# A hybrid transformer block: x given a second time by channel, parameters as one array of columns

## The chip, the cores and the metric

The kernel runs on one core of a Trainium2 chip. The metric is the device time of one execution in microseconds. Engines are written as the profile writes them: PE (TensorE), PEld (its weight loads), DVE (VectorE), ACT (ScalarE), POOL (GpSimd), SP (SyncE, which here only issues transfers).

## The reference, cut to what matters

One decoder block on x of 512 tokens by 2048 channels, float32. The first part, which the change touches:

```
h      = x * rsqrt(mean(x*x over channels) + EPS) * mix_pre_g      # RMSNorm
proj   = h @ w_in                                                  # 2048 -> 7168
a_in, b_in, gates = split(proj)
a      = causal_depthwise_conv(a_val * sigmoid(a_gate), conv_a_w, 31 taps) + conv_a_b
a      = silu(layernorm(a) * ln_a_g + ln_a_b);   y_a = a @ w_a_out
y_b    = (causal pooling of b_in, one 256x256 map per group) * pool_scale @ w_b_out
x      = x + rmsnorm((sigmoid(g_a)*y_a + sigmoid(g_b)*y_b) @ w_o, mix_post_g)
```

Then come a gated MLP (2048 to 2 x 5632 and back, convolution of 3 taps, GELU) and a gated per-layer embedding, each with RMSNorm before or after it and a residual sum. Output: 512 by 2048 float32.

## The kernel before, in words

Every float32 product is made of three matmuls on float32r operands: each operand is split into a high part (rounded by ACT) and a low part (the rest, subtracted by DVE), and PE computes high x high, high x low and low x high (`products`, L732, lines 734 to 736). An output tile is 128 output channels by 512 tokens, a PSUM bank; the contraction goes over 16 chunks of 128 channels, so channels must lie on partitions: chunk c of x is `xg_hi[:, c]` and `xg_lo[:, c]`, 128 channels by 512 tokens, already multiplied by the gain `mix_pre_g` of its channel. The token's factor (one over the root of the mean square) is applied to the results, not to x.

Weights come in units of 128 x 1024 (512 KB): for `w_in` a unit is half a column of tiles, 8 chunks of 128 x 128. A unit is loaded by SP into one of 2 raw slots (`load`, L460; a slot is free when the unit two before it has been split, `lo_ready`), split by ACT (`split`, L1027) and by DVE (`split`, L1431) into one of 4 slots, and used by PE. In the following, w0, w1, ... are the units in order. The orders of all engines are written out by hand and meet at semaphores; one engine's instructions run strictly in order.

The start of the kernel, by engine:

- SP (L480 to L489): x rows group 0 (512 tokens by 512 channels, 1 MB, tokens on partitions, `x_nat[:, 0]`), w0 and w1, x rows groups 1 to 3, then w2 and w3 (each waits for its raw slot), then w4 and on in a loop. All these go into one queue.
- ACT issues the load of `mix_pre_g`, and within its loop (L1103) those of the other parameters, as rows.
- PE (L821 to L835) turns the gain with the identity matrix, then runs `first_pair` (L769): two output tiles side by side (banks 0 and 1), chunk by chunk, 6 matmuls a chunk. `turn` (L760) transposes one chunk of x with four 128 x 128 matmuls; 4 chunks are turned ahead of chunk 0, and 4 more ahead of chunks 2, 6 and 10. Chunks 0 to 7 use w0 and w1, chunks 8 to 15 use w2 and w3. Then 7 transpositions put the other parameters on partitions. Then the third tile (w4 and w5): chunks 0 to 7 with w4, then `spread(1, 7)` (L813), which broadcasts the token factors over partitions with PE and waits for `diag_ready`, then chunks 8 to 15 with w5. Then the fourth tile (w6 and w7), and so on.
- ACT (L1096 to L1114): makes `xg_hi[:, c]` for c from 0 to 15 out of PSUM; splits w0 after c = 0, w1 after c = 1, w2 after c = 7, w3 after c = 8 (`FIRST_SPLITS`); then w4 and w5 (`step`, each also waits until w0 or w1 was used up); then the squares of x by rows, one instruction for each of four blocks of tokens, with sums (`row_squares_of`, L1053), the square root (`standard_deviation`, L1050), then w6 and w7.
- DVE (L1514 to L1533): `xg_lo[:, c]`, the low parts of the units in the same order, the parameters out of PSUM, the reciprocals and the diagonal matrices for `spread` (`token_factors`, `diagonals`), the low parts of w6 and w7, the copy of the spread factors to `r_bc`, which every later result is multiplied by.

Of the kernel before, what the change touches and what calls it, by code (L numbers as in the profile page):

```python
# [28 lines left out]
F32 = mybir.dt.float32  # L29
# [202 lines left out]

def build(nc, x, p_t, mix_pre_g, w_in, conv_a_w, conv_a_b, ln_a_g, ln_a_b, w_a_out, pool_w, pool_scale, w_b_out,
          w_o, mix_post_g, ffn_pre_g, w_up, conv_f_w, conv_f_b, w_down, ffn_post_g, w_ple, w_ple_gate,
          ple_post_g, out):
    x2_dram = nc.dram_tensor("x2_dram", (P, NG, BLK, W), F32, kind="Internal").ap()
# [4 lines left out]
    with ctx:  # L241
# [10 lines left out]
        def place(name, shape, dt, offset):  # L252
            return nc.alloc_sbuf_tensor_at(name, shape, dt, offset=offset)
# [55 lines left out]

        par_nat = place("par_nat", [P, 7, P], F32, r5)  # L310
        gain0_nat = place("gain0_nat", [DC, P], F32, r5 + 4096)
        squares_out = place("squares_out", [P, NG, W], F32, r5 + D * 4)
# [68 lines left out]
        consts_ready, ident_zero, table_loaded = sem("consts_ready"), sem("ident_zero"), sem("table_loaded")  # L381
        par_turned, par_ready = sem("par_turned"), sem("par_ready")

# [71 lines left out]
        def _(sp):  # L455
# [11 lines left out]
            def half_column(u, w, col, h):  # L467

                load(u, w[:, 8 * h:8 * h + 8, bass.ds(col, P)], P)
# [5 lines left out]
            def rows(u, w, k, n):  # L475

                load(u, w[:, bass.ds(k, 2), bass.ds(n * W, W)], W)

            xr = rows_of(x)
            sp.dma_start(x_nat[:, 0], xr[:, 0]).then_inc(x_in[0], 16)  # L480
            for j in range(2):
                half_column(At(U_A + j), win, (H, 0)[j], 0)
            for n in range(1, NG):
                sp.dma_start(x_nat[:, n], xr[:, n]).then_inc(x_in[n], 16)
            for j in range(2):
                half_column(At(U_A + 2 + j), win, (H, 0)[j], 1)
            with sp.Fori(1, HC) as c:
                column(At(U_A, c, 4), win, c * P + H)
                column(At(U_A + 2, c, 4), win, c * P)  # L489
# [234 lines left out]
        def _(pe):  # L724
# [17 lines left out]
            def chunk_products(o, u, k, hi, lo, chunks):  # L742

                last = products(o, u.slot(SLOTS), slice(k % 8 * P, (k % 8 + 1) * P), hi[:, k], lo[:, k], k == 0, k == chunks - 1)
                if k % 8 == 7:
                    last.then_inc(units_done, 1)
# [13 lines left out]
            def turn(src, base, c, bank0):  # L760
# [6 lines left out]
                mm.then_inc(turned, 1)  # L767

            def first_pair(u, src, base, arrived, tile_bank, turn_bank):  # L769

                def turns(n):
                    if n < NG:
                        arrived(n)
                        for c in range(4 * n, 4 * n + 4):
                            turn(src, base, c, turn_bank)
                turns(0)
                for k in range(DC):
                    if k % 4 == 2:
                        turns(k // 4 + 1)
                    pe.wait_ge(turned_split, base + k + 1)  # L780
                    for j in range(2):
                        if k % 8 == 0:
                            pe.wait_ge(lo_ready, u + 2 * (k // 8) + j + 1)
                        chunk_products(ps[:, tile_bank + j], At(u + 2 * (k // 8) + j), k, xg_hi, xg_lo, DC)

# [34 lines left out]

            pe.wait_ge(par_in0, 16)  # L821
            pe.transpose(ps[:, 2, 0:DC], gain0_nat[:], ident[0:DC, 0:DC]).then_inc(par_turned, 1)
            first_pair(U_A, x_nat, 0, lambda n: pe.wait_ge(x_in[n], 16), 0, 4)
            pe.wait_ge(par_in1, 16 * 12)
            n = CONV_W * HC // 2
            pe.transpose(ps[:, 5, 0:C_CAW], par_nat[0:C_CAW, 0], ident[0:C_CAW, 0:C_CAW])
            for j in range(2):
                pe.transpose(ps[:, 5, C_CAW + j * n:C_CAW + (j + 1) * n], par_nat[0:n, 1 + j], ident[0:n, 0:n])
            n = 2 * FC
            for j in range(1 + FTAPS):  # L830
                mm = pe.transpose(ps[:, 6, j * n:(j + 1) * n], par_nat[0:n, 3 + j], ident[0:n, 0:n])
            mm.then_inc(par_turned, 1)
            pe.wait_ge(par_ready, 1)
            tile(At(U_A + 4), At(T_A + 2), xg_hi, xg_lo, between=lambda: spread(1, 7))
# [189 lines left out]
        def _(act):  # L1024
# [20 lines left out]
            def step(u, ahead=True):  # L1045
                act.wait_ge(units_done, (u + 1).value())
                if ahead:
                    split(u + SLOTS)
# [4 lines left out]
            def row_squares_of(src, done):  # L1053

                for b in range(BLK):
                    if done + b > 0:
                        act.wait_ge(row_squares, done + b)
                    f(squares_out[:], src[:, :, b], ACT.Square, accum_out=row_sum[:, b:b + 1]).then_inc(row_squares, 1)
                act.wait_ge(row_squares, done + BLK)

            def turned_high(base, c, bank0, dst, scale):
                act.wait_ge(turned, base + c + 1)
                f(dst[:, c], ps[:, bank0 + c % 4], ACT.Identity, scale=scale).then_inc(turned_hi, 1)
# [17 lines left out]
            def param(base, q):  # L1081

                return par[:, q.c + base:q.c + base + 1] if q.i is None else par[:, bass.ds(q.i * q.k + (q.c + base), 1)]

            as_rows = lambda v: v.rearrange("(c p) -> c p", p=P)
            act.dma_start(gain0_nat[:], as_rows(mix_pre_g)).then_inc(par_in0, 16)
            act.wait_ge(consts_ready, 3)
            load_table(ACT.Identity)
            taps = conv_a_w.rearrange("k (c p) -> (k c) p", p=P)
            n = CONV_W * HC // 2  # L1090
            params = [(par_nat[col:col + v.shape[0] // P, 0], as_rows(v)) for col, v in
                      ((C_FFNPRE, ffn_pre_g), (C_CAB, conv_a_b), (C_LNG, ln_a_g), (C_LNB, ln_a_b), (C_PSC, pool_scale), (0, mix_pre_g))]
            params += [(par_nat[0:n, 1 + j], taps[j * n:(j + 1) * n]) for j in range(2)]
            params += [(par_nat[0:2 * FC, 3], as_rows(conv_f_b))]
            params += [(par_nat[0:2 * FC, 4 + k], as_rows(conv_f_w[k])) for k in range(FTAPS)]
            act.wait_ge(par_ready, 1)  # L1096
            for c in range(DC):
                turned_high(0, c, 4, xg_hi, par[:, C_MIXPRE + c:C_MIXPRE + c + 1])
                if c in FIRST_SPLITS:
                    split(At(FIRST_SPLITS.index(c)))  # L1100
                if c in (3, 7):
                    for to, src in params[0:6] if c == 3 else params[6:]:
                        act.dma_start(to, src).then_inc(par_in1, 16)  # L1103
            for k in range(2):
                step(At(U_A + k))
            row_squares_of(x_nat, 0)
            standard_deviation(D, row_sum[:])
# [314 lines left out]
        def _(dve):  # L1422
# [90 lines left out]

            dve.wait_ge(par_turned, 1)  # L1514
            dve.tensor_copy(par[:, 0:DC], ps[:, 2, 0:DC]).then_inc(par_ready, 1)
            dve.wait_ge(par_ready, 1)
            for c in range(DC):
                dve.wait_ge(turned_hi, c + 1)
                scaled_low(xg_lo[:, c], ps[:, 4 + c % 4], param(C_MIXPRE, At(c)), xg_hi[:, c], turned_split)
                if c in FIRST_SPLITS:  # L1520
                    split(At(FIRST_SPLITS.index(c)))
            for k in range(2):
                step(At(U_A + k))
            dve.wait_ge(par_turned, 2)
            op(dve.tensor_copy(par[:, DC:C_CFB], ps[:, 5, DC:C_CFB]))
            dve.tensor_copy(par[:, C_CFB:C_ALL], ps[:, 6, 0:C_ALL - C_CFB]).then_inc(par_ready, 1)
            dve.wait_ge(par_ready, 2)
            dve.wait_ge(consts_ready, 3 + PPAD)
# [338 lines left out]
            def sum_7():  # L1867

                dve.wait_ge(x2_out, 16)
                dve.wait_ge(row_squares, 2 * BLK)  # L1870
                dve.wait_ge(turned, 2 * DC)
                op(dve.tensor_tensor(s7_raw[:], s3_raw[:], part(xg_hi, first_half, near), ALU.subtract))
                op.settle()
                dve.tensor_tensor(s7_raw[:], s7_raw[:], part(xg_lo, first_half, near), ALU.subtract).then_inc(s_ready, 1)
# [318 lines left out]

NAMES = ["x", "p", "mix_pre_g", "w_in", "conv_a_w", "conv_a_b", "ln_a_g", "ln_a_b", "w_a_out", "pool_w", "pool_scale",
         "w_b_out", "w_o", "mix_post_g", "ffn_pre_g", "w_up", "conv_f_w", "conv_f_b", "w_down", "ffn_post_g", "w_ple",
         "w_ple_gate", "ple_post_g"]

# [23 lines left out]
```

## Time and profile before

| | |
|---|---|
| median of 3 runs | 2572.82 us (2571.35 to 2573.98) |
| profiled execution, its own time | 2572.78 us |
| its span, first to last instruction | 2571.0 us |
| mean granted TensorE clock | 0.993 |
| PE busy | 2522.8 us, 98% |
| DVE busy | 1828.5 us, 71% |
| ACT busy | 1021.7 us, 40% |
| HBM | 379.67 MB read, 36.96 MB written |

The profile is of one execution; its times are microseconds from the first instruction. The time of the execution is 1.8 us more than the span.

### The profile page before, as it was taken

The page shows a single profiled execution, that of the slowest core. Times are in us where ns is not written, and L with a number is a line of the kernel's source. Part 1 is how long each engine was busy: PE and PEld are TensorE (multiplying, and loading weights), DVE is VectorE, ACT ScalarE, POOL GpSimd, SP SyncE. Part 2 cuts the span into 40 slices and gives each one's busy share as a digit, 9 for nine tenths or more (in the row PEclk, how much of TensorE's full clock was granted, in tenths as well). Part 3 has the DMA queues.
Part 4 walks back from the last instruction along what each step waited for, and adds up shares of the span by engine and source line. Part 5 has one row for each costly group of instructions (what it writes and reads, how often), then busy time and mean ns, then how long its engine had stood idle before and what let it go on. Part 6 is the DMA issues. An engine that isn't in the chain of part 4 may idle for free.

```text
span 2571.0 us, 36185 instructions
## 1 busy us (share of the span) xinstructions
PE 2522.8 (98%) x14322; PEld 2218.3 (86%) x14322; DVE 1828.5 (71%) x2216; ACT 1021.7 (40%) x1188; POOL 184.7 (7%) x261
## 2 busy tenths in 40 slices
PE   8999999999999999999999999999999999998998
PEld 7888888888888888899999999999987878876886
DVE  6888766653334236889889999899998786877434
ACT  5222322252223224444444454444454544545323
POOL 0000000000000000011111111111111101200000
PEclk9999999999999999999999999999999999999999
DMA  5333333333333423467777777677797777955221
GB/s 164 104 98 98 99 99 98 90 115 98 93 96 118 144 98 132 145 186 219 204 190 212 218 210 209 185 216 220 205 288 235 260 236 212 303 169 192 94 99 66
DMA packets 255054, 418.72 MB, mean 163 GB/s; under 512 B 12820, under 2 KB 161980, under 8 KB 253884
## 3 DMA queue, kind: packets, MB, share of 16 engines
q1 hardware_dynamic: 221056, 293.64, 34.6%
q0 software_dynamic: 30928, 118.50, 19.3%
q10 hardware_dynamic: 2924, 4.54, 0.5%
q8 instruction: 102, 1.67, 0.3%
q14 instruction: 44, 0.36, 0.1%
HBM read 379.67 MB, written 36.96 MB: 162 GB/s over the span
## 4 chain that ended last, share of the span: by engine, by line
PE 89%; DVE 5%; DMA 2%; issue 2%; ACT 1%; POOL 0%; DVEq 0%; ACTq 0%; SPq 0%
PE ps L734 10%; PE ps L736 10%; PE ps L735 10%; PE ps L945 10%; PE ps L943 10%; PE ps L944 10%; PE ps L985 5%; PE ps L805 5%; PE ps L987 5%; PE ps L986 5%; PE ps L806 5%; PE ps L807 5%; DMA ring_raw<-in_w_down 1%; DVE x L1503 1%; DVE ring_lo L1449 1%
## 5 line engine op out<-in xcount | busy, mean ns | idle before, releaser
L1043 ACT ACTIVATE w_hi<-ring_raw 128x1024 fp32r<-128x1024 f32 x426 | 451.1, 1060 | 626.8 <-PE ps L945 391.1
L1449 DVE TENSOR_TENSOR ring_lo<-ring_raw,w_hi 128x1024 fp32r<-128x1024 f32 x426 | 518.3, 1221 | 202.7 <-ACT w_hi L1043 201.1
L1438 DVE TENSOR_TENSOR w_lo<-w_raw,w_hi 128x1024 fp32r<-128x1024 f32 x194 | 236.8, 1223 | 409.4 <-ACT w_hi L1033 409.0
L1033 ACT ACTIVATE w_hi<-w_raw 128x1024 fp32r<-128x1024 f32 x194 | 204.9, 1059 | 528.5 <-PE ps L736 387.4
L734 PE MATMUL ps<-xg_hi,w_hi 128*128 128x512 f32 x1024 | 400.5, 391 | 0.7 <-DVE w_lo L1438 0.6
L736 PE MATMUL ps<-xg_hi,w_lo 128*128 128x512 f32 x1024 | 399.1, 390 | 0.0
L735 PE MATMUL ps<-xg_lo,w_hi 128*128 128x512 f32 x1024 | 399.0, 390 | 0.0
L943 PE MATMUL ps<-s_hi,w_hi 128*128 128x256 f32 x1280 | 362.7, 283 | 3.2 <-issue 3.2
L945 PE MATMUL ps<-s_hi,ring_lo 128*128 128x256 f32 x1280 | 362.9, 284 | 0.0
L944 PE MATMUL ps<-s_lo,w_hi 128*128 128x256 f32 x1280 | 362.5, 283 | 0.0
L943 PE MATMUL ps<-xg_hi,w_hi 128*128 128x256 f32 x960 | 271.1, 282 | 0.4 <-DVE ring_lo L1449 0.4
L945 PE MATMUL ps<-xg_hi,ring_lo 128*128 128x256 f32 x960 | 271.3, 283 | 0.0
L944 PE MATMUL ps<-xg_lo,w_hi 128*128 128x256 f32 x960 | 271.0, 282 | 0.0
L985 PE MATMUL ps<-w_hi,xd 128*128 128x512 f32 x608 | 240.1, 395 | 15.9 <-DVE cb L2054 8.4
L943 PEld LDWEIGHTS ps<-s_hi,w_hi 128*128 128x128 f32 x1280 | 244.8, 191 | 3.3 <-issue 3.3
L945 PEld LDWEIGHTS ps<-s_hi,ring_lo 128*128 128x128 f32 x1280 | 247.0, 193 | 0.0
L944 PEld LDWEIGHTS ps<-s_lo,w_hi 128*128 128x128 f32 x1280 | 245.0, 191 | 0.0
L986 PE MATMUL ps<-w_hi,xd 128*128 128x512 f32 x608 | 238.9, 393 | 0.0
L734 PEld LDWEIGHTS ps<-xg_hi,w_hi 128*128 128x128 f32 x1024 | 192.6, 188 | 41.1 <-issue 1.0
L736 PEld LDWEIGHTS ps<-xg_hi,w_lo 128*128 128x128 f32 x1024 | 192.6, 188 | 40.4
L735 PEld LDWEIGHTS ps<-xg_lo,w_hi 128*128 128x128 f32 x1024 | 192.7, 188 | 39.6
L987 PE MATMUL ps<-ring_lo,xd 128*128 128x512 f32 x520 | 204.4, 393 | 0.0
(243 smaller groups left out, 4205.5 us busy)
## 6 DMA issues: line engine op xcount, KB each, us to landing
ring_raw<-in_w_up SPq DMA_DIRECT2D x200, 512.0 KB, 5.0
ring_raw<-in_w_down SPq DMA_DIRECT2D x114, 512.0 KB, 4.6
w_raw<-in_w_in SPq DMA_DIRECT2D x112, 512.0 KB, 3.8
ring_raw<-in_w_up POOLq DMA_DIRECT2D x80, 512.0 KB, 6.1
w_raw<-in_w_o SPq DMA_DIRECT2D x32, 512.0 KB, 3.6
ring_raw<-in_w_ple_gate SPq DMA_DIRECT2D x32, 512.0 KB, 3.6
xd_raw<-gx_dram POOLq DMA_DIRECT2D x14, 1024.0 KB, 10.6
gx_dram<-g_sums POOLq DMA_DIRECT2D x44, 256.0 KB, 9.1
```

Source lines behind the costliest of these rows:

```text
L734: pe.matmul(o, w_hi[:, s, cols], hi, start=start, stop=False)
L735: pe.matmul(o, w_hi[:, s, cols], lo, start=False, stop=False)
L736: return pe.matmul(o, w_lo[:, s, cols], hi, start=False, stop=stop)
L943: pe.matmul(o, w_hi[:, s, cols], hi(k), start=k == 0, stop=False)
L944: pe.matmul(o, w_hi[:, s, cols], lo(k), start=False, stop=False)
L945: mm = pe.matmul(o, w_low[:, cols], hi(k), start=False, stop=k == HC - 1)
L985: pe.matmul(o, x_tile[:, 0, tok], w_hi[:, s, cols], start=first and k == 0, stop=False)
L986: pe.matmul(o, x_tile[:, 1, tok], w_hi[:, s, cols], start=False, stop=False)
L987: mm = pe.matmul(o, x_tile[:, 0, tok], w_low[:, cols], start=False, stop=final and k == 1)
L1043: f(w_hi[:, (U_S + n) % SLOTS], raw_of(n), ACT.Copy).then_inc(hi_ready, 1)
L1438: dve.tensor_tensor(w_lo[:, s], w_raw[:, u.slot(RAW)], as_f32(w_hi[:, s]), ALU.subtract).then_inc(lo_ready, 1)
L1449: dve.tensor_tensor(low_of_unit(n), raw_of(n), as_f32(w_hi[:, (U_S + n) % SLOTS]), ALU.subtract).then_inc(lo_ready, 1)
```

## The change

The kernel is given two more arrays, laid out on the host, in place of nine parameter vectors and matrices: `x_t`, which is x as [channel within its chunk, chunk, token], and `columns`, all per-channel parameters as 128 rows of 664. The array x by rows stays.

SP loads `x_t` in eight pieces of two chunks (512 KB each): piece 0, w0, w1, pieces 1 to 7, w2, w3, and then the four groups of x by rows (1 MB each), then w4 and on. ACT issues two loads of `columns` at the start (8 KB and 332 KB). PE has no transposition ahead of or within the first pair and none for parameters. ACT and DVE read the chunks of x from SBUF instead of PSUM; ACT waits for the rows of x after it has split w4 and w5, ahead of the squares.

```diff
-        par_nat = place("par_nat", [P, 7, P], F32, r5)
-        gain0_nat = place("gain0_nat", [DC, P], F32, r5 + 4096)
+        xt_raw = place("xt_raw", [P, DC, TOK], F32, r3)
...
+            def turned_x(k):
+
+                sp.dma_start(xt_raw[:, 2 * k:2 * k + 2], x_t[:, 2 * k:2 * k + 2]).then_inc(xt_in[k], 16)
+
             xr = rows_of(x)
-            sp.dma_start(x_nat[:, 0], xr[:, 0]).then_inc(x_in[0], 16)
+            turned_x(0)
             for j in range(2):
                 half_column(At(U_A + j), win, (H, 0)[j], 0)
-            for n in range(1, NG):
-                sp.dma_start(x_nat[:, n], xr[:, n]).then_inc(x_in[n], 16)
+            for k in range(1, DC // 2):
+                turned_x(k)
             for j in range(2):
                 half_column(At(U_A + 2 + j), win, (H, 0)[j], 1)
+            for n in range(NG):
+                sp.dma_start(x_nat[:, n], xr[:, n]).then_inc(x_in[n], 16)
             with sp.Fori(1, HC) as c:
...
+            def first_products(u, base, k, tile_bank):
+
+                pe.wait_ge(turned_split, base + k + 1)
+                for j in range(2):
+                    if k % 8 == 0:
+                        pe.wait_ge(lo_ready, u + 2 * (k // 8) + j + 1)
+                    chunk_products(ps[:, tile_bank + j], At(u + 2 * (k // 8) + j), k, xg_hi, xg_lo, DC)
...
-            pe.wait_ge(par_in0, 16)
-            pe.transpose(ps[:, 2, 0:DC], gain0_nat[:], ident[0:DC, 0:DC]).then_inc(par_turned, 1)
-            first_pair(U_A, x_nat, 0, lambda n: pe.wait_ge(x_in[n], 16), 0, 4)
-            pe.wait_ge(par_in1, 16 * 12)
-            n = CONV_W * HC // 2
-            pe.transpose(ps[:, 5, 0:C_CAW], par_nat[0:C_CAW, 0], ident[0:C_CAW, 0:C_CAW])
-            for j in range(2):
-                pe.transpose(ps[:, 5, C_CAW + j * n:C_CAW + (j + 1) * n], par_nat[0:n, 1 + j], ident[0:n, 0:n])
-            n = 2 * FC
-            for j in range(1 + FTAPS):
-                mm = pe.transpose(ps[:, 6, j * n:(j + 1) * n], par_nat[0:n, 3 + j], ident[0:n, 0:n])
-            mm.then_inc(par_turned, 1)
-            pe.wait_ge(par_ready, 1)
+            for k in range(DC):
+                first_products(U_A, 0, k, 0)
             tile(At(U_A + 4), At(T_A + 2), xg_hi, xg_lo, between=lambda: spread(1, 7))
...
-            act.dma_start(gain0_nat[:], as_rows(mix_pre_g)).then_inc(par_in0, 16)
+            act.dma_start(par[:, 0:DC], columns[:, 0:DC]).then_inc(par_in0, 16)
+            act.dma_start(par[:, DC:C_ALL], columns[:, DC:C_ALL]).then_inc(par_in1, 16)
             act.wait_ge(consts_ready, 3)
             load_table(ACT.Identity)
...
-            act.wait_ge(par_ready, 1)
+            act.wait_ge(par_in0, 16)
             for c in range(DC):
-                turned_high(0, c, 4, xg_hi, par[:, C_MIXPRE + c:C_MIXPRE + c + 1])
+                if c % 2 == 0:
+                    act.wait_ge(xt_in[c // 2], 16)
+                f(xg_hi[:, c], xt_raw[:, c], ACT.Identity, scale=par[:, C_MIXPRE + c:C_MIXPRE + c + 1]).then_inc(turned_hi, 1)
                 if c in FIRST_SPLITS:
                     split(At(FIRST_SPLITS.index(c)))
-                if c in (3, 7):
-                    for to, src in params[0:6] if c == 3 else params[6:]:
-                        act.dma_start(to, src).then_inc(par_in1, 16)
             for k in range(2):
                 step(At(U_A + k))
+            for n in range(NG):
+                act.wait_ge(x_in[n], 16)
             row_squares_of(x_nat, 0)
             standard_deviation(D, row_sum[:])
...
-            dve.wait_ge(par_turned, 1)
-            dve.tensor_copy(par[:, 0:DC], ps[:, 2, 0:DC]).then_inc(par_ready, 1)
-            dve.wait_ge(par_ready, 1)
+            dve.wait_ge(par_in0, 16)
             for c in range(DC):
                 dve.wait_ge(turned_hi, c + 1)
-                scaled_low(xg_lo[:, c], ps[:, 4 + c % 4], param(C_MIXPRE, At(c)), xg_hi[:, c], turned_split)
+                scaled_low(xg_lo[:, c], xt_raw[:, c], param(C_MIXPRE, At(c)), xg_hi[:, c], turned_split)
...
-            dve.wait_ge(par_turned, 2)
-            op(dve.tensor_copy(par[:, DC:C_CFB], ps[:, 5, DC:C_CFB]))
-            dve.tensor_copy(par[:, C_CFB:C_ALL], ps[:, 6, 0:C_ALL - C_CFB]).then_inc(par_ready, 1)
-            dve.wait_ge(par_ready, 2)
+            dve.wait_ge(par_in1, 16)
```

The counts that other stages wait for (`turned`) start 16 lower; nothing else in the later stages differs.

## Rows read from the trace of the kernel before

**Rows 1.** The page: busy times of the engines, and the chain that ended last.
```profile
PE 2522.8 (98%) x14322; PEld 2218.3 (86%) x14322; DVE 1828.5 (71%) x2216; ACT 1021.7 (40%) x1188; POOL 184.7 (7%) x261
...
PE 89%; DVE 5%; DMA 2%; issue 2%; ACT 1%; POOL 0%; DVEq 0%; ACTq 0%; SPq 0%
```
**Rows 2.** The chain of waits in the first 50 us: start, length, what.
```profile
15.35 1.75 PE ps L766 x16
...
39.78 0.20 PE ps L826
39.98 0.36 PE ps L828 x2
40.34 0.31 PE ps L831 x4
40.65 0.27 PE ps L734
40.91 0.23 PE ps L735
...
46.15 0.89 PE ps L817 x8
47.04 0.23 PE ps L734
```
**Rows 3.** Timeline of PE: start, length, line, operation, idle before in brackets.
```profile
12.03 0.80 PE L734 MATMUL ps<-xg_hi,w_hi 128*128 128x512 f32 x1
12.62 0.63 PE L735 MATMUL ps<-xg_lo,w_hi 128*128 128x512 f32 x1
```
**Rows 4.** Timeline of ACT, first 50 us.
```profile
7.87 1.05 ACT L1033 ACTIVATE w_hi<-w_raw 128x1024 fp32r<-128x1024 f32 x1
...
19.84 1.06 ACT L1033 ACTIVATE w_hi<-w_raw 128x1024 fp32r<-128x1024 f32 x1 [1.59 <-DMA w_raw<-in_w_in]
...
34.50 1.92 ACT L1058 ACTIVATE squares_out<-x_nat 128x2048 f32<-128x2048 f32 x1
```
**Rows 5.** Timeline of DVE, first 50 us.
```profile
20.93 1.23 DVE L1438 TENSOR_TENSOR w_lo<-w_raw,w_hi 128x1024 fp32r<-128x1024 f32 x1 [1.66 <-ACT w_hi L1033]
...
44.56 0.88 DVE L1485 TENSOR_SCALAR diag<-ident,rstd 128x128 f32<-128x128 f32 x4
45.36 2.35 DVE L1438 TENSOR_TENSOR w_lo<-w_raw,w_hi 128x1024 fp32r<-128x1024 f32 x2
```
**Rows 6.** Busy time by stretch; the last three columns: granted clock, DMA share, GB/s.
```profile
0.00:3.00 3.00, 0.00 (x0) 0.00 (x0) 0.00 (x0) 1.49 (x2) 1.40 (x24) 1.00 0.33 45
3.00:5.00 2.00, 0.26 (x1) 0.18 (x1) 0.17 (x1) 0.00 (x0) 0.00 (x0) 1.00 1.05 402
6.00:8.00 2.00, 1.93 (x9) 1.93 (x10) 0.00 (x0) 0.71 (x2) 0.00 (x0) 1.00 1.19 296
10.00:17.00 7.00, 6.59 (x29) 5.15 (x30) 3.75 (x6) 2.98 (x6) 0.00 (x0) 1.00 1.06 385
18.00:20.00 2.00, 2.00 (x11) 1.62 (x10) 1.27 (x2) 0.41 (x2) 0.00 (x0) 1.00 1.20 291
```
**Rows 7.** Timeline of the queue's issues by SP, first 60 us.
```profile
2.42 5.25 SPq L484 DMA_DIRECT2D x_nat<-in_x  x3
10.28 47.16 SPq L465 DMA_DIRECT2D w_raw<-in_w_in  x9
```
**Rows 8.** Timeline of PE: three idle times late in the kernel.
```profile
2263.97 0.80 PE L985 MATMUL ps<-w_hi,xd 128*128 128x512 f32 x1 [4.92 <-DVE cb L2054]
...
2326.73 0.50 PE L985 MATMUL ps<-w_hi,xd 128*128 128x512 f32 x1 [3.45 <-DVE cb L2054]
...
2359.78 0.79 PE L805 MATMUL ps<-w_hi,p_hi 128*128 128x512 f32 x1 [2.85 <-ACT e_buf L1379]
```
**Rows 9.** By stretch, as Rows 6: after the first and third of these, and two wider ones.
```profile
2263.97:2266.87 2.90, 2.90 (x7) 2.32 (x8) 2.90 (x3) 0.00 (x0) 0.00 (x0) 0.50 0.19 75
2359.78:2366.50 6.72, 6.72 (x17) 5.28 (x18) 5.98 (x8) 4.87 (x8) 0.00 (x0) 0.54 0.01 5
...
50.00:80.00 30.00, 30.00 (x134) 24.83 (x133) 29.69 (x43) 7.52 (x8) 0.00 (x0) 1.00 0.30 89
47.00:100.00 53.00, 53.00 (x236) 43.85 (x235) 47.64 (x68) 12.84 (x14) 0.00 (x0) 1.00 0.38 110
```

More of the change, by code:

```diff
@@ L230, in leave, with build @@
         self.at = At(self.base + n * per)
-def build(nc, x, p_t, mix_pre_g, w_in, conv_a_w, conv_a_b, ln_a_g, ln_a_b, w_a_out, pool_w, pool_scale, w_b_out,
-          w_o, mix_post_g, ffn_pre_g, w_up, conv_f_w, conv_f_b, w_down, ffn_post_g, w_ple, w_ple_gate,
-          ple_post_g, out):
+def build(nc, x, x_t, columns, p_t, w_in, w_a_out, pool_w, w_b_out, w_o, mix_post_g, w_up, w_down, ffn_post_g, w_ple,
+          w_ple_gate, ple_post_g, out):
     x2_dram = nc.dram_tensor("x2_dram", (P, NG, BLK, W), F32, kind="Internal").ap()
@@ L381, in build @@
         consts_ready, ident_zero, table_loaded = sem("consts_ready"), sem("ident_zero"), sem("table_loaded")
-        par_turned, par_ready = sem("par_turned"), sem("par_ready")
+        xt_in = [sem(f"xt_in{k}") for k in range(DC // 2)]
         turned, turned_hi, turned_split = sem("turned"), sem("turned_hi"), sem("turned_split")
@@ L779, in first_pair @@
                         turns(k // 4 + 1)
-                    pe.wait_ge(turned_split, base + k + 1)
-                    for j in range(2):
-                        if k % 8 == 0:
-                            pe.wait_ge(lo_ready, u + 2 * (k // 8) + j + 1)
-                        chunk_products(ps[:, tile_bank + j], At(u + 2 * (k // 8) + j), k, xg_hi, xg_lo, DC)
+                    first_products(u, base, k, tile_bank)
             def rows(u, t, bank0, x_hi, x_lo, chunks, wait=None, ahead=None, by_block=0):
@@ L818, in spread @@
                 mm.then_inc(spread_done, 1)
-            pe.wait_ge(par_in0, 16)
-            pe.transpose(ps[:, 2, 0:DC], gain0_nat[:], ident[0:DC, 0:DC]).then_inc(par_turned, 1)
-            first_pair(U_A, x_nat, 0, lambda n: pe.wait_ge(x_in[n], 16), 0, 4)
-            pe.wait_ge(par_in1, 16 * 12)
-            n = CONV_W * HC // 2
-            pe.transpose(ps[:, 5, 0:C_CAW], par_nat[0:C_CAW, 0], ident[0:C_CAW, 0:C_CAW])
-            for j in range(2):
-                pe.transpose(ps[:, 5, C_CAW + j * n:C_CAW + (j + 1) * n], par_nat[0:n, 1 + j], ident[0:n, 0:n])
-            n = 2 * FC
-            for j in range(1 + FTAPS):
-                mm = pe.transpose(ps[:, 6, j * n:(j + 1) * n], par_nat[0:n, 3 + j], ident[0:n, 0:n])
-            mm.then_inc(par_turned, 1)
-            pe.wait_ge(par_ready, 1)
+            for k in range(DC):
+                first_products(U_A, 0, k, 0)
             tile(At(U_A + 4), At(T_A + 2), xg_hi, xg_lo, between=lambda: spread(1, 7))
@@ L1061, in turned_high @@
             def turned_high(base, c, bank0, dst, scale):
-                act.wait_ge(turned, base + c + 1)
+                act.wait_ge(turned, base - DC + c + 1)
                 f(dst[:, c], ps[:, bank0 + c % 4], ACT.Identity, scale=scale).then_inc(turned_hi, 1)
@@ L1083, in param @@
                 return par[:, q.c + base:q.c + base + 1] if q.i is None else par[:, bass.ds(q.i * q.k + (q.c + base), 1)]
-            as_rows = lambda v: v.rearrange("(c p) -> c p", p=P)
-            act.dma_start(gain0_nat[:], as_rows(mix_pre_g)).then_inc(par_in0, 16)
+            act.dma_start(par[:, 0:DC], columns[:, 0:DC]).then_inc(par_in0, 16)
+            act.dma_start(par[:, DC:C_ALL], columns[:, DC:C_ALL]).then_inc(par_in1, 16)
             act.wait_ge(consts_ready, 3)
             load_table(ACT.Identity)
[L1089 to L1095, printed above, removed]
-            act.wait_ge(par_ready, 1)
+            act.wait_ge(par_in0, 16)
             for c in range(DC):
-                turned_high(0, c, 4, xg_hi, par[:, C_MIXPRE + c:C_MIXPRE + c + 1])
+                if c % 2 == 0:
+                    act.wait_ge(xt_in[c // 2], 16)
+                f(xg_hi[:, c], xt_raw[:, c], ACT.Identity, scale=par[:, C_MIXPRE + c:C_MIXPRE + c + 1]).then_inc(turned_hi, 1)
                 if c in FIRST_SPLITS:
                     split(At(FIRST_SPLITS.index(c)))
-                if c in (3, 7):
-                    for to, src in params[0:6] if c == 3 else params[6:]:
-                        act.dma_start(to, src).then_inc(par_in1, 16)
             for k in range(2):
                 step(At(U_A + k))
+            for n in range(NG):
+                act.wait_ge(x_in[n], 16)
             row_squares_of(x_nat, 0)
@@ L1870, in sum_7 @@
                 dve.wait_ge(row_squares, 2 * BLK)
-                dve.wait_ge(turned, 2 * DC)
+                dve.wait_ge(turned, DC)
                 op(dve.tensor_tensor(s7_raw[:], s3_raw[:], part(xg_hi, first_half, near), ALU.subtract))
@@ L2191, in _ @@
             finish(3)
-NAMES = ["x", "p", "mix_pre_g", "w_in", "conv_a_w", "conv_a_b", "ln_a_g", "ln_a_b", "w_a_out", "pool_w", "pool_scale",
-         "w_b_out", "w_o", "mix_post_g", "ffn_pre_g", "w_up", "conv_f_w", "conv_f_b", "w_down", "ffn_post_g", "w_ple",
-         "w_ple_gate", "ple_post_g"]
+NAMES = ["x", "x_t", "columns", "p", "w_in", "w_a_out", "pool_w", "w_b_out", "w_o", "mix_post_g", "w_up", "w_down",
+         "ffn_post_g", "w_ple", "w_ple_gate", "ple_post_g"]
+COLUMNS = ["mix_pre_g", "ffn_pre_g", "conv_a_b", "ln_a_g", "ln_a_b", "pool_scale", "conv_a_w", "conv_f_b", "conv_f_w"]
 def kernel(**inputs):
@@ L2205 @@
     for name in NAMES:
-        a = np.ascontiguousarray(inputs[name])
+        if name == "columns":
+            a = np.concatenate([np.asarray(inputs[k]).reshape(-1, P) for k in COLUMNS]).T
+        elif name == "x_t":
+            a = np.asarray(inputs["x"]).reshape(TOK, DC, P).transpose(2, 1, 0)
+        else:
+            a = inputs[name]
+        a = np.ascontiguousarray(a)
         if name == "w_up":
```

## The prediction, on record before the change ran

> **What bounds the kernel now.** I read the page first: PE is busy for 98% of the span, and 89% of the chain that ended last is PE's [rows 1]. So only what makes PE shorter, or makes it wait, can move the time. The change touches the first 50 us, and there I read the chain of waits, the timelines of ACT, DVE and SP, and the bytes moved in each stretch. The chain shows one unbroken run of PE from 12.03 us on: matmuls 0.23 us apart, groups of 16 transpositions (1.75 us each, at 15.35, 22.59 and 29.83; one of the three stands in the rows), seven transpositions of parameters from 39.78 to 40.65, 24 matmuls of the third tile, and at 46.15 the spreading of the token factors [rows 2]. The DVE timeline shows how near that last step is to another limit: the diagonal matrices that it waits for were done at 44.56 + 0.88 = 45.44 [rows 5], 0.7 us before PE came to it. Everything ahead of them is one chain on ACT: the squares of x by rows begin at 34.50 [rows 4], and from there to 45.44 are 10.94 us. The reader should see that work taken from PE ahead of 46.15 is worth no more than 0.7 us unless this chain gets earlier too.
>
> **The change, part by part.** *PE loses* three groups of transpositions, 3 x 1.75 = 5.25 us, and the parameter transpositions, 40.65 - 39.78 = 0.87 us [rows 2]: 6.1 us. The first group and the gain's stand ahead of the first product and are in its start.
>
> *The start.* I date transfers by bytes. Up to 3.00 us 3 x 45 GB/s = 0.135 MB had moved; after it x moves at 385 GB/s (1 MB loads of x, pieces of 2 KB) and weights at (296 + 291)/2 = 293 GB/s [rows 6], one after the other as SP queued them. A test on the kernel before: ahead of and with w2 go 4.194 MB of x and 1.573 MB of weights: 3.00 + 4.059/0.385 + 1.573/0.293 = 18.9 us, and ACT, which was waiting for w2, starts on it at 19.84 [rows 4]. So 0.93 us lie between the last byte and the reader. In the new order w1 has x_t piece 0 (0.524 MB), the columns (0.340 MB), w0 and itself before it: 3.00 + 0.729/0.385 + 1.049/0.293 + 0.93 = 9.4 us. ACT's split (1.06) and DVE's (1.22) follow: PE's unbroken run begins at about 11.7 instead of 12.03, a gain of 0.3 us. The first products ran at 0.63 us where later ones take half the time per result [rows 3]; without transpositions ahead of them I give the slow matmuls 1 to 2 us more. That time is spent ahead of a wait below and costs nothing.
>
> What the array does at its start is a place where the Trainium skill speaks against the change: "TensorE: Matmul & The Clock Gate", on the clock gate, says that the throttled clock is the default and that activity releases it, and the 16 transpositions ahead of the first product were such activity. By that rule the first pair ends up to 2 us later; the sum below stays the same, since PE has 2.4 us to spare there.
>
> *Chunks 0 to 15.* ACT and DVE make a chunk in 0.7 us each, PE uses one in 6 x 0.23 = 1.4 us, and two chunks of x_t arrive each 0.524/0.385 = 1.4 us, so nothing is late until w2 and w3. These land at 20.7 and 22.5 (0.340 MB of columns later than before); w3's low part is ready at 24.8, PE comes to it at 24.5, and the pair ends at about 35.0, where before it was 39.78. The 0.332 MB of parameters are needed only at DVE's wait after the low parts of w4 and w5, 20 us after they landed.
>
> *What is moved: x by rows, and with it the third tile and the squares.* Four loads of 1 MB stand in the queue ahead of w4 and w5. SP issues them right after w3, when w1's raw slot is split, near 12 us; it can put more than 3 MB in the queue ahead of the data, as its three loads of x issued by 7.67 us show [rows 7], and w4 is issued when it has room and w2's slot is free (22 us). The queue never runs dry, so bytes date w5: x twice 8.389 MB, columns 0.340 MB, six units 3.146 MB: 3.00 + (8.729 - 0.135)/0.385 + 3.146/0.293 + 0.93 = 37.0 us. w4 is 1.8 us ahead of it, 35.2. Before, w5 had landed by the time ACT wanted it (the squares start at 34.50 right after its split).
> - PE: w4's low part at 35.2 + 1.06 + 1.22 = 37.5, a wait of 2.5 us; then 24 matmuls, 46.15 - 40.65 = 5.5 us: PE comes to the spreading at 43.0.
> - ACT: w5 split 37.0 to 38.0, and the same 10.94 us to the end of the diagonals: 48.9. PE waits 6 us and goes on at 48.9 where before it did at 46.15, or 46.0 by the timeline: 2.9 us later.
> Behind the waiting ACT stand w6 and w7 (split right after the root, low part by DVE by 51.4; PE wants w6 at about 56) and the copy of the spread factors; DVE is busy 29.69 of 30 us from 50 to 80 [rows 9], and moves by the same 3 to 3.5 us, less than PE will, so it adds no wait.
>
> *The clock after the wait.* In this trace 4.92 us of idle PE were followed by 2.90 us at a granted clock of 0.50, that is 1.2 GHz; 2.85 us of idle by 6.72 us at 0.54; 3.45 us of idle by matmuls that ran at full speed [rows 8, 9]. Half of each is lost: 1.5, about 3.1, and nothing. Of an idle time of 6 us I take 1.7 us, one short stretch, with 0 and 3.4 as bounds.
>
> **The sum.** +2.9 + 1.7 = +4.6 us: from the profiled execution's 2572.78 us (span 2571.0 and 1.8 around it) to 2577.4. That execution is at the median of the runs shown, 2572.82. Everything behind 50 us is the same and paced by PE, so the delay stays. Bounds: bytes at the best rates that the rows show for x, 402 GB/s [rows 6], take 0.9 us off; with no slow clock the result is +2.0; with a long slow stretch +6.3. I cannot bound the speed of x_t's 4 KB pieces by a row of its own kind; between 293 and 402 GB/s it is worth +3.4 to -0.4 us, and I take 385 since the rate in this trace goes with the size of the piece in memory (2 KB against 512 B), and 4 KB is nearer to the first.
>
> **Rivals.**
> - *Slower, x_t at the rate of small loads.* Every 512 KB load in the trace moves at 293 GB/s, and x_t comes in 512 KB loads. Then its 4.194 MB take 14.3 instead of 10.9 us, w5 lands 3.4 us later, and all of it reaches PE: +8.0, 2580.8 us. It decides as soon as x_t is slower than about 370 GB/s. For it: the size of the load. Against it: the weights come in pieces of 512 B. The Trainium skill, "DMA: Bandwidth & Descriptors", Bandwidth, backs it: it advises loads of 1 MiB or more and gives 78% of the peak for one such load.
> - *Slower, a long stretch at half clock after the wait.* As after 2359.78 [rows 9]: +2.9 + 3.4 = +6.3, 2579.1 us.
> - *No loss: the squares start early.* If bytes move at 402 GB/s (x) and 320 GB/s (weights), w5 lands at 35 and PE goes on 0.9 us later than before, with or without a short slow stretch: about 2573.7 to 2575; and if something in my chain is pessimistic by 1 us, 2572.8. Against it: no stretch of weights is above 296 GB/s.
> - *Faster: PE's removed work is the gain.* 6.1 + 0.3 = 6.4 us off, 2566.4 us. It needs the diagonals by 46.0 - 6.4 = 39.6 and so w5 and the rows by 27.7 us, 11.9 MB in 25 us, 480 GB/s; no row is above 402. It could still come if part of the chain does not hold as I read it, for instance if PE does not pause at the spreading.
>
> **How the numbers follow.** Forecast 0.50, 2577.4 us (its own range 2575.5 to 2578.5); long slow clock 0.18; x_t slow 0.14; no loss 0.11; faster 0.07. A measurement of this kernel tells about 0.2%, 5.1 us, from no change. Slower than that: 0.32 for two rivals and a sixth of the forecast's 0.50, so 0.40; faster 0.07; within it 0.53. The range leaves out the faster case and the ends of the slow ones: 2573.5 to 2581.0.
>
> **What would show it.** Right: no transposition ahead of 900 us; w4's high part starts at 35 to 36 us on ACT after a wait for its transfer; the squares start at about 38; PE has an idle time of 2 to 3 us ahead of the third tile and one of about 6 us ahead of the spreading, ended by the diagonals at 49; matmuls at 0.63 us behind it. Wrong: squares that start before 35 us, or PE without an idle time ahead of the spreading; then the gain of 6 us stands. If x_t lands slower than one piece in 1.6 us, the first slower rival holds. If the first 60 us come out as I say but the time differs by more than 3 us, something later depends on when this stage ends, which I hold to be excluded.

## The result, and the profile after

The changed kernel takes 2577.7 us (median of 17 runs, 2574.32 to 2581.59) against 2572.91 us (17 runs, 2571.35 to 2574.51) before: 4.8 us more, ratio 1.002 with a 95% interval of 1.0013 to 1.0027, that is 3.3 to 6.9 us. The forecast was 2577.4 us. The profiled execution has a span of 2579.8 us, 8.8 more than the one before. Of these, 5.3 are made in the first 60 us; the rest comes late in the kernel and, as a second profile will show, belongs to that one execution.

The page of the changed kernel: PE lost 72 transpositions (64 of x, 8 of parameters) and 3.6 us of busy time, and the span grew all the same.

```profile
span 2579.8 us, 36032 instructions
...
PE 2519.2 (98%) x14250; PEld 2213.3 (86%) x14250; DVE 1828.0 (71%) x2213; ACT 1023.6 (40%) x1188; POOL 184.9 (7%) x261
```

This is the chain of waits in its first 60 us (start, length, what; `...` marks lines left out). Where the kernel before has PE in an unbroken run [rows 2], the chain now hangs on transfers up to 37 us, then on ACT's squares, then on DVE's diagonals, and comes to PE only at the spreading (L825 here, L817 before). The transfer from 24.46 on is w5: 12.49 us from issue to landing, nearly all of it in the queue behind the rows of x and w4.

```profile
9.94 10.15 DMA w_raw<-in_w_in
...
24.46 12.49 DMA w_raw<-in_w_in
...
38.00 2.00 ACT squares_out L1055 x2
...
48.06 0.89 DVE diag L1476 x4
...
48.99 2.08 PE ps L825 x8
```

This is the timeline of ACT in the same stretch. The entries in brackets are idle time and what ended it. ACT waits 8.33 us for w4, then the squares follow w5 at 38.00, 3.5 us later than in [rows 4].

```profile
20.12 1.06 ACT L1030 ACTIVATE w_hi<-w_raw 128x1024 fp32r<-128x1024 f32 x1 [5.64 <-DMA w_raw<-in_w_in]
...
35.57 1.06 ACT L1030 ACTIVATE w_hi<-w_raw 128x1024 fp32r<-128x1024 f32 x1 [8.33 <-DMA w_raw<-in_w_in]
37.04 1.06 ACT L1030 ACTIVATE w_hi<-w_raw 128x1024 fp32r<-128x1024 f32 x1 [0.42 <-DMA w_raw<-in_w_in]
...
38.00 1.90 ACT L1055 ACTIVATE squares_out<-x_nat 128x2048 f32<-128x2048 f32 x1
```

This is the timeline of PE: its start, the wait for w4's low part, the wait for the diagonals, and the first products behind it at 0.63 us, where they take 0.39 once the clock is full.

```profile
11.69 0.79 PE L738 MATMUL ps<-xg_hi,w_hi 128*128 128x512 f32 x1
...
15.27 0.63 PE L740 MATMUL ps<-xg_hi,w_lo 128*128 128x512 f32 x1
...
16.36 0.40 PE L740 MATMUL ps<-xg_hi,w_lo 128*128 128x512 f32 x1
...
37.94 0.50 PE L738 MATMUL ps<-xg_hi,w_hi 128*128 128x512 f32 x1 [2.81 <-DVE w_lo L1429]
...
48.99 2.08 PE L825 MATMUL ps<-diag,ones 128*128 128x128 f32 x8 [5.31 <-DVE diag L1476]
...
50.72 0.77 PE L738 MATMUL ps<-xg_hi,w_hi 128*128 128x512 f32 x1
51.29 0.63 PE L739 MATMUL ps<-xg_lo,w_hi 128*128 128x512 f32 x1
```

These are the bytes and the clock by stretch, columns as in [rows 6]. x_t moves at 410 GB/s, the rows of x at 386, w4 and w5 at 280; around the spreading the granted clock is 0.57. The last two rows show that almost everything had moved by 35 us.

```profile
10.00:17.00 7.00, 6.91 (x17) 5.00 (x18) 5.61 (x8) 4.26 (x7) 0.00 (x0) 1.00 1.03 410
22.00:31.00 9.00, 9.00 (x41) 7.44 (x41) 6.87 (x10) 5.24 (x8) 0.00 (x0) 1.00 1.05 386
33.00:35.00 2.00, 2.00 (x10) 1.43 (x8) 0.00 (x0) 0.00 (x0) 0.00 (x0) 1.00 1.11 280
46.00:54.00 8.00, 5.01 (x17) 4.35 (x18) 5.92 (x12) 5.38 (x8) 0.00 (x0) 0.57 0.29 84
0.00:35.00 35.00, 24.93 (x96) 19.70 (x96) 15.41 (x20) 15.88 (x22) 1.40 (x24) 1.00 1.02 338
35.00:37.00 2.00, 0.12 (x1) 0.00 (x0) 0.34 (x1) 1.06 (x1) 0.00 (x0) 1.00 0.11 29
```

### The profile page after: what moved, and what is told of

It is laid out like the page before. It is cut to its first block, busy times and chain, and to the rows that moved or that the text cites. A ratio compares the mean times of both kernels' runs of the same rounds, so it can differ in the third digit from the quotient of the medians.

```text
span 2579.8 us, 36032 instructions
## 1 busy us (share of the span) xinstructions
PE 2519.2 (98%) x14250; PEld 2213.3 (86%) x14250; DVE 1828.0 (71%) x2213; ACT 1023.6 (40%) x1188; POOL 184.9 (7%) x261
## 4 chain that ended last, share of the span: by engine, by line
PE 92%; DVE 3%; DMA 2%; issue 1%; ACT 1%; POOL 0%; DVEq 0%; SPq 0%; ACTq 0%
PE ps L740 11%; PE ps L738 11%; PE ps L739 11%; PE ps L942 10%; PE ps L940 10%; PE ps L941 10%; PE ps L982 5%; PE ps L984 5%; PE ps L983 5%; PE ps L813 5%; PE ps L814 5%; PE ps L815 5%; DMA w_raw<-in_w_in 1%; DMA ring_raw<-in_w_down 1%; PE ps L770 1%
```

## The experiments

To part what happens in the first stage from what happens later, I use one marker: the first of PE's transpositions of the second x, some 994 us into the kernel. These are its lines in the timeline of PE, in this order: the kernel before, the changed kernel, and the experiments on which a verdict rests most (unaltered again; rows behind w5; without rows; busy in both waits; squares by channel).

```profile
993.95 3.53 PE L766 MATMUL ps<-ident,x 128*128 128x128 f32 x16 [2.61 <-DVE x L1503]
```
```profile
999.23 3.57 PE L770 MATMUL ps<-ident,x 128*128 128x128 f32 x16 [2.62 <-DVE x L1494]
```
```profile
999.30 3.48 PE L770 MATMUL ps<-ident,x 128*128 128x128 f32 x16 [2.61 <-DVE x L1494]
```
```profile
1003.09 3.01 PE L772 MATMUL ps<-ident,x 128*128 128x128 f32 x16 [2.62 <-DVE x L1496]
```
```profile
989.52 2.90 PE L768 MATMUL ps<-ident,x 128*128 128x128 f32 x16 [2.61 <-DVE x L1490]
```
```profile
997.17 3.29 PE L770 MATMUL ps<-ident,x 128*128 128x128 f32 x16 [2.62 <-DVE x L1500]
```
```profile
988.09 3.18 PE L772 MATMUL ps<-ident,x 128*128 128x128 f32 x16 [2.61 <-DVE x L1509]
```

"Marker" is this start less 993.95, "span" the profile's span less 2571.0; the medians are of all timed runs, the ratio is to the kernel before on the same chip. The kernel before had medians of 2572.91 us beside the first row, 2572.37 beside the next four, 2574.59 beside "no rows" and "squares by channel", and 2572.83 beside the last two, so ratios compare better than medians.

| run | median us | ratio, 95% interval | marker | span |
|---|---|---|---|---|
| changed kernel, as above | 2577.7 | 1.002, 1.0013 to 1.0027 | +5.3 | +8.8 |
| the same again | 2578.21 | 1.0022, 1.0013 to 1.0032 | +5.4 | +5.2 |
| rows unread | 2576.7 | 1.0017, 1.0008 to 1.0026 | +4.5 | +0.7 |
| rows behind w5 | 2581.36 | 1.0034, 1.0022 to 1.0046 | +9.1 | +13.4 |
| kept busy, second wait | 2574.41 | 1.001, 1.0001 to 1.0019 | +4.2 | +1.4 |
| no rows | 2566.37 | 0.9971, 0.9959 to 0.9984 | -4.4 | -6.3 |
| squares by channel | 2564.5 | 0.9962, 0.9948 to 0.9975 | -5.9 | -5.2 |
| busy in both waits | 2575.26 | 1.0009, 1.0 to 1.0018 | +3.2 | +1.8 |
| columns alone | 2572.43 | 0.9998, 0.9989 to 1.0007 | 0.0 | -0.4 |

**The changed kernel again.** No edit.

> The changed kernel unaltered, for a second profile. Its first profile lies 8.8 us above that of the kernel before, its median only 4.8 us. If the delay is made in the first 60 us (5.3 us in the first profile: 2.9 to 3.3 us of chain and 2 of slow clock) and the rest came from slow-clock stretches that fall differently in each execution, the delay at 60 us comes out at 3 to 6.5 us again, and the later part differs from 3.5 us, by up to 3 us either way. If the rest is a lasting effect of the change on later stages, it comes out at 3.5 us again, with the same waits grown. Median 2577 to 2578 either way.

The marker is the same within 0.1 us, but behind it this execution lies 0.2 us under the kernel before where the first lay 3.5 us over it. So the lasting delay is the first stage's, and the other 3.5 us were that execution's. The traces show where they came in: 0.9 us by the first matmul behind the wait of 4.9 us late in the kernel [rows 8] (2270.20 us against 2263.97, less the 5.3), and 2.6 us behind it, where the clock granted over 130 us was lower than in the other two executions. The rows are of the kernel before, of the changed kernel, and of the changed kernel again:

```profile
2255.00:2385.00 130.00, 115.31 (x496) 93.01 (x495) 100.24 (x104) 60.82 (x94) 7.11 (x11) 0.96 0.56 179
2255.00:2385.00 130.00, 116.09 (x481) 93.36 (x480) 99.11 (x99) 61.39 (x91) 7.66 (x12) 0.93 0.54 176
2255.00:2385.00 130.00, 115.31 (x488) 92.82 (x487) 101.89 (x103) 62.25 (x92) 7.64 (x12) 0.96 0.56 184
```

**Rows loaded but not read.** ACT takes the squares from x_t.

```diff
+            row_squares_of(xt_raw.rearrange("p (n b) t -> p n b t", b=BLK), 0)
             for n in range(NG):
                 act.wait_ge(x_in[n], 16)
-            row_squares_of(x_nat, 0)
```

> Changed kernel, x by rows still loaded at the same place in the queue, but ACT takes the squares from x_t, which landed long before, in the same four instructions and at the same place in its order, and waits for the rows only behind them (the token factors are wrong by this). Theory 1, that w4 and w5 queued behind the rows set the start of the squares: nothing changes, squares start at 38, median 2577.7. Theory 2, that the rows' own arrival sets it: squares start before 37 and the median falls by 1 us or more.

The squares start at 38.02 and the spreading at 48.99, as in the changed kernel. What is late is not the data that the squares read; it is w4 and w5, which ACT must split first and which stand behind the rows in the queue. (The marker is 0.8 us less because the slow clock fell in other places. Eight matmuls ran slowly behind PE's first wait, which only shortened the second one, to 3.71 us; behind the second wait the slow stretch was shorter than in the changed kernel.)

**Rows behind w5.**

```diff
+            column(At(U_A + 4), win, P + H)
             for n in range(NG):
                 sp.dma_start(x_nat[:, n], xr[:, n]).then_inc(x_in[n], 16)
-            with sp.Fori(1, HC) as c:
+            column(At(U_A + 6), win, P)
+            with sp.Fori(2, HC) as c:
```

> Changed kernel, the four loads of rows queued behind w5 instead of ahead of w4. Theory 1, bytes: the same bytes stand ahead of the squares, w5 lands at 28 but the rows at 38, so the squares start at 38 to 38.5; PE's wait ahead of the third tile goes, that ahead of the spreading grows from 5.3 to 8 us; median 2577.5 to 2579. Theory 2, that the late w4 costs PE its 2.8 us: the median falls by 2.8 us to 2575.

Neither number came. The wait ahead of the third tile is gone, as expected, but the squares start at 41.13, not 38, and the marker is 3.8 us worse. The bytes by stretch say why: from 21 to 24 us the queue is empty. w4's load may be issued only when w2 has been split, its data come from 24 us on, and in this order nothing stands ahead of it to fill the time. In the changed kernel the rows fill just that hole. The first row shows the hole, the second the clock around the spreading, at half from end to end.

```profile
21.00:24.00 3.00, 3.00 (x14) 2.03 (x12) 2.67 (x3) 3.00 (x6) 0.00 (x0) 1.00 0.05 15
45.00:58.00 13.00, 5.88 (x18) 5.01 (x19) 6.61 (x13) 10.11 (x13) 0.00 (x0) 0.50 0.26 73
```

These are ACT's wait for the rows and PE's for the diagonals in this run:

```profile
41.13 1.91 ACT L1057 ACTIVATE squares_out<-x_nat 128x2048 f32<-128x2048 f32 x1 [10.08 <-DMA x_nat<-in_x]
...
52.12 2.07 PE L827 MATMUL ps<-diag,ones 128*128 128x128 f32 x8 [11.76 <-DVE diag L1478]
```

Counting bytes dates a transfer only while the queue is never empty; that condition held for the changed kernel and not here. The rival, that w4's lateness costs PE 2.8 us by itself, falls: with w4 in time PE only came earlier to the diagonals and waited 11.76 us for them.

**PE kept busy ahead of the spreading, then in both waits.**

```diff
+            def busy(n):
+
+                for _ in range(n):
+                    pe.matmul(ps[:, 7], xg_hi[:, 0, 0:P], xg_hi[:, 1], start=True, stop=True)
+
+            busy(11)
-            tile(At(U_A + 4), At(T_A + 2), xg_hi, xg_lo, between=lambda: spread(1, 7))
+            tile(At(U_A + 4), At(T_A + 2), xg_hi, xg_lo, between=lambda: [busy(21), spread(1, 7)])
```

The edit shown is that of the second of the two. The first has 22 matmuls in the second wait and none in the first.

> Changed kernel with 22 matmuls of 128x512 more, on data at hand and into the bank of the spreading, issued by PE ahead of its wait for the diagonals, where it was idle for 5.3 us; they take 22 x 0.227 = 5.0 us. If the slow clock behind the wait is a part of the loss (1.7 us in the prediction, 2.0 in the first profile), the granted clock stays at 1.00 there and the median falls by 1.5 to 2.5 us to about 2575.7, with less spread between runs. If the clock is no part of it, or the added matmuls are late, the median stays or rises by up to 1 us.

The sign is right, the placing was not: the first wait, left idle, was now followed by a short stretch at half clock, PE was late by that, and the 22 matmuls ended at 50.2, 1.2 us behind the diagonals. The spreading began at 50.19 and took 1.05 us, as in the kernel before. Hence the second, with both waits filled:

> Changed kernel, with matmuls of 128x512 on data at hand in both waits: 11 (2.5 us) ahead of the third tile, 21 (4.8 us) ahead of the spreading, so that PE is not idle for more than 1 us and neither list ends behind its wait. If the loss in the first 60 us is chain plus slow clock, no slow stretch falls before 60 us and the delay there is the chain's alone, 3.0 to 3.5 us instead of 5.3; median 1.5 to 2.5 us under that of the changed kernel. If the added matmuls delay the spreading, the delay stays at 4 us or more.

```profile
34.29 2.65 PE L834 MATMUL ps<-xg_hi 128*128 128x512 f32 x11
...
43.62 4.92 PE L834 MATMUL ps<-xg_hi 128*128 128x512 f32 x21
...
49.10 1.16 PE L825 MATMUL ps<-diag,ones 128*128 128x128 f32 x8 [0.56 <-DVE diag L1482]
```

The spreading starts when it did (49.10), takes 1.16 us instead of 2.08, and the marker falls from +5.3 to +3.2. So by the marker the chain costs 3.2 us and the clock 2.1. The ratios (1.0022 and 1.0009) differ by 3.3 us; their intervals overlap, so the marker carries this verdict.

**No rows.** The four loads left out, squares of x_t as above.

> Changed kernel without the loads of x by rows; ACT takes the squares from x_t in the same four instructions at the same place (the token factors are wrong by this). Theory 1, bytes ahead of w5: w4 lands near 26.5 and w5 near 28, the squares start near 30, the diagonals are ready near 41, when PE comes to the spreading at about 41 too; PE goes on 5 us earlier than in the kernel before, median 2567 to 2568.5. The rival, that the removed transpositions are worth nothing even without the wait (something later paces this stage): median 2572 to 2573.

The squares start at 30.48, the diagonals still hold PE up for 1.2 us, and the marker is 4.4 us under the kernel before. The shorter PE is worth most of its time once the transfer is gone. The ratio gives more, 7.5 us (4.1 to 10.6); its interval holds the marker's 4.4.

**Squares by channel, a version that computes everything.** Every chunk of x_t is squared by ACT, in its idle time ahead of w2 and behind w5; DVE adds them; one matmul with ones gives the sums on all partitions.

```diff
+                pe.matmul(ps[:, 7], ones[:], sq_sum[:, 0], start=True, stop=True).then_inc(spread_done, 1)
...
+                    f(x_sq[:, c], xt_raw[:, c], ACT.Square).then_inc(x_sq_ready, 1)
...
+                if c == 7:
+                    chunk_squares(range(8))
...
-            row_squares_of(x_nat, 0)
-            standard_deviation(D, row_sum[:])
+            chunk_squares(range(8, DC))
+            for k in range(2, 4):
+                step(At(U_A + k))
+            load_table(ACT.Sqrt)
+            act.wait_ge(spread_done, 1)
+            f(std_bc[:], ps[:, 7], ACT.Sqrt, bias=eps[:], scale=1.0 / D).then_inc(std_ready, 1)
```

> The whole result, without x by rows: squares of x_t by ACT chunk by chunk (8 in its idle time ahead of w2, 8 behind w5), summed by DVE, and the sums over channels spread by one matmul with ones, which gives the token factors on all partitions with no diagonals. ACT splits w6 and w7 ahead of the root. PE should not wait at all between 12 us and the end of the fourth tile: 6.1 us less than before of transpositions, a start 0.3 us earlier, some 0.8 us more of slow matmuls at the start. Expected 5 to 6 us under the kernel before, median 2567 to 2568, the same as without rows and wrong factors. If DVE, with 15 additions and a reciprocal of 128x512 more, becomes late after 45 us, PE waits for banks or low parts and the median is 2569 or more.

It is faster than both kernels: 0.9962 of the kernel before, 0.9948 to 0.9975. The chain of its first 60 us is PE's again from 11.4 us on, with no wait at the matmul with ones (L836):

```profile
11.41 0.80 PE ps L740
...
40.31 0.86 PE ps L836 x2
```

The ratio says 9.8 us (6.4 to 13.4), the marker 5.9 and the span 5.2; the expected 5 to 6 us are what the profile shows. The distance to the ratio comes from the executions compared: the profiled one took 2567.72 us, 3.2 more than this kernel's median, and the kernel before had a median of 2574.59 beside it, 1.8 more than its own profiled execution. With five runs, the marker's 5.9 us is the figure to go by. The feared cost on DVE is there and hidden: the reciprocal of 128x512 took 3.35 us, and no wait of PE was added in these 60 us.

```profile
41.93 3.35 DVE L1548 RECIPROCAL r_bc<-std_bc 128x512 f32<-128x512 f32 x1 [2.62 <-ACT std_bc L1115]
```

**Columns alone.** The kernel before with the parameters as columns and x still turned by PE.

> Kernel before with the other part of the change alone: all parameters as columns (the 332 KB of them loaded where the parameter rows were loaded before), no parameter transpositions; x is still turned by PE. PE is 0.87 us shorter ahead of the spreading, where it had 0.7 us to spare against the diagonals. My theory: the gain is 0.7 us or less, with PE coming to the spreading at 45.3 and waiting up to 0.2 us there; median within 1 us of the kernel before. The rival, that parameters without transpositions move the whole stage: 2 us or more.

```profile
45.86 1.16 PE L816 MATMUL ps<-diag,ones 128*128 128x128 f32 x8 [0.31 <-DVE diag L1463]
```

PE now comes to the spreading early and waits 0.31 us for the diagonals; it goes on 0.13 us earlier than before, and the marker does not move. The 0.87 us taken from PE bring nothing that shows at the marker or in the median, which is the reading on which the forecast rested. The test is a little blunter than planned: this execution started some 0.35 us late (the squares at 34.85 against 34.50, the diagonals done at 45.80 against 45.44). Whether by the edit or by chance is not shown. With the start of before, PE would have gone on about 0.5 us earlier (an estimate: 0.13 + 0.36), still under the 0.7.

## Why the prediction was right

- *What bounds the stage.* Predicted: work taken from PE is worth at most 0.7 us, because the diagonals come 0.7 us ahead of PE. Columns alone shows PE waiting for the diagonals as soon as its work is 0.87 us shorter.
- *The bytes.* Predicted w4's split at 35 to 36 and the squares at 38; measured 35.57 and 38.00. The one rate without a row, x_t's, was taken as 385 GB/s and is 410, so the first slower rival (512 KB loads at 293 GB/s, 2580.8 us) falls: x_t and the weights both come in loads of 512 KB and moved at 410 and 280. What went with the rate in these traces is the size of the piece in memory: 4 KB at 410, 2 KB at 386, 512 B at 280. That w5's reader came out at 37.0 (measured 37.04) is in part luck. Of the 11.875 MB up to w5, 35 x 338 GB/s = 11.83 had moved by 35.0 us, where the sum has the last byte at 36.1; and ACT started on w5 2.0 us after that, where the sum allows 0.93. Both terms were about 1 us off, in opposite directions. In those 2 us the DMA share is 0.11, so a few transfers were still running; which ones is not shown.
- *The chain term.* Predicted +2.9; the spreading starts at 48.99 against 45.99, +3.0, and +3.2 at the marker with the clock kept up. Rows unread and rows behind w5 tie it to the order of the queue, and without the rows it is gone.
- *PE's waits.* Predicted 2.5 and 6.0 us, measured 2.81 and 5.31. The second is shorter because PE came at 43.7, not 43.0. The slow matmuls at the start, forecast at 1 to 2 us more, came too: they take 0.63 us up to 15.7 us (before: up to 13.9), though the column of the granted clock says 1.00 there. The first pair ended at 35.13, and as forecast the wait for w4 hid this.
- *The clock term.* Predicted 1.7 with 0 and 3.4 as bounds, measured 2.1. This was the weakest term. The three waits elsewhere had cost 1.5, about 3.1 and 0 us, from which neither the 1.7 nor the bound of 3.4 comes out; 1.7 was a choice between them, and the experiments show both shorter and longer slow stretches after these waits. So that the size came near is luck; that a slow stretch costs time here is shown by filling the waits.
- *The sum.* Predicted +4.6, in the profiles +5.3 at the marker, in the medians +4.8. That is within my bound of 0.2% (5.1 us), near its edge, and the interval reaches beyond it (3.3 to 6.9 us). The interval of the ratio lies clear of 1, so 17 runs do tell this loss from no change.
- *The side that I gave 0.07*, PE's removed work as a gain of 6.4 us, failed for the reason given: the rows' bytes ahead of w5. Without these bytes 4.4 us of it show at the marker; the wait of 1.2 us that is left at the spreading and about 0.9 us of slower matmuls at the start account for the rest.

## What to carry to other kernels

Ahead of work taken from the busiest engine, look at the next step at which it meets another chain, and at how long before it that chain is done: the gain is no more than the smaller of the work taken away and this margin. Bytes added to a queue delay everything queued behind them, also what has nothing to do with them (here w4 and w5). Date a transfer by summing bytes, and check that the queue does not run dry. If the moved input is only needed for a reduction that another copy can give, drop it instead of moving it.

## What the runs showed of the hardware

Later in the kernel the same work met a slow clock in one execution and not in another. In the stretch around 1100 us and in that around 2360 us the granted clock was 0.83 in the kernel before and 1.00 with both waits filled. The first fence is of the kernel before, the second of the kernel with both waits filled.

```profile
1095.00:1115.00 20.00, 17.30 (x122) 17.16 (x123) 12.61 (x15) 6.28 (x8) 6.11 (x8) 0.83 0.58 158
2355.00:2375.00 20.00, 16.46 (x61) 12.70 (x60) 11.52 (x17) 11.59 (x20) 0.53 (x1) 0.83 0.16 54
```
```profile
1095.00:1115.00 20.00, 17.00 (x140) 16.45 (x138) 13.37 (x15) 5.36 (x8) 6.11 (x8) 1.00 0.59 179
2355.00:2375.00 20.00, 18.71 (x82) 14.97 (x82) 16.15 (x25) 12.45 (x22) 0.00 (x0) 1.00 0.23 79
2255.00:2385.00 130.00, 116.87 (x487) 93.95 (x486) 100.54 (x103) 60.08 (x90) 7.64 (x12) 0.93 0.56 178
```

At 0.83 over 20 us, 6.8 us are at half speed, 3.4 us lost. Nothing in either kernel differs there, and the two executions of the changed kernel have 0.83 in both stretches. The two places are not alike, though. Around 1100 us the slow clock was truly absent: between the marker and the first matmul behind the long wait near 2264 us the kernel with both waits filled gained 2.1 us on the kernel before (it starts that matmul 1.2 us later, the marker 3.2 us later). Around 2360 us it only fell elsewhere: over the 130 us from 2255 on the clock is 0.93 there, against 0.96 in the kernel before, so a narrow stretch alone misleads. What decides where it falls was not found. The two executions of the changed kernel differ by 3.6 us in span with no cause in the code, so differences of a few microseconds are to be read at a marker near the change and not from the spans.
